# The GLU product of a state-space branch as three split products, and a reordered turn between two phases of an attention stage

## Chip, cores and metric

The kernel runs on one core of one Trainium2 chip. The metric is device time in microseconds, from the start of the one launch to its end. Three runs of the kernel before took 1898.04, 1898.96 and 1899.64 us (median 1898.96).

## What is computed

One layer of a decoder trunk over 2048 tokens with D_MODEL = 1024. An input projection feeds three causal mixers (pooling, forgetting attention with 8 heads of 64, a complex-diagonal state-space layer), each with its own gate; they are merged with sigmoid gates, projected and normalised.

```python
z = einsum('bsd,de->bse', x, w_in) + b_in      # zc: state branch; q, k, v, f: attention; zg: merge gates
# state branch, u = zc (256 channels)
y = Re(C x_t) + D * u                          # x_t = Abar x_{t-1} + Bbar u_t, 16 groups of 16 channels
y = gelu(y)
y_c = y * sigmoid(y @ w_glu + b_glu) * silu(gc)         # w_glu: 256 x 256
# attention, per head
p = softmax(q k^T / 8 + F[t] - F[s], causal);  y_b = (p @ v) * silu(gb)
gates = sigmoid(zg);  merged = sum_i gates_i * (y_i @ w_up_i)
out = layer_norm(2**0.25 * x + merged @ w_out)
```

## The kernel before

All products on TensorE (PE) that matter are split products: each fp32 operand is written as a high part in fp32r (ScalarE, ACT, copies and rounds) and a low part in fp32r (VectorE, DVE, subtracts), and high*high, high*low and low*high are added in PSUM. The low part lies where the raw fp32 operand lay (`low_with_raw`).

**Stage 1, projection** (`stage_project`, to 599 us). The tokens are taken in two halves of 1024 (`hf`), 24 weight tiles of 128 columns each. A tile is 48 matmuls of 128x512 (8 depth blocks, 3 split products, 2 banks). Two PSUM tiles, two weight buffers. Between the tiles PE does small products for the side branches, in PSUM banks `aux_ps`. At the end of a half, for the state branch: `y` products, a tile, 16 transposes into `yT` (which lies over `u_sb`), a tile, then `glu()` (L897 to L907), which multiplies `w_glu` with `yT` in plain fp32, 8 matmuls of 128x512. ACT applies GELU (L398) to `yT` before that. In the first half the tile ahead of `glu()` is the last one that reads the first half of x, so x of the second half is loaded, split by ACT (L355) and DVE (L451) at the same time. In the second half one tile follows `glu()` (`project_halves`).

**Stage 2, attention** (`stage_attend`, 600 to 1529 us). A loop over 8 heads. Every head is one written-out order on PE (`head`): `queries` (q k^T of one block of 128 queries into `s_ps`), `turn` (128x128 transposes of the weights `s_sb` into `t_ps`), `values` (times v into `o_ps`), and between them `fill`: matmuls of the gate projection, 6 tiles of 48 per head, so 24 tiles in 4 heads. Heads 0 to 3 (phase 0) take the gate tiles of one half of the tokens, heads 4 to 7 (phase 1) those of the other. At the change of phase x of the other half is loaded again (SP, L1249) and split again: ACT L1387, DVE L1504, 16 pieces of 128x512 each. In the first tile of phase 1 PE waits for each depth block of x_lo (`fresh`, in `fill`). A head begins with q k^T of block 0 and the transposes of v (L1629, into both `t_ps`). ACT then splits gate weights (L1346), copies the high part of v (L1394), and takes the exponential of block t (L1400) once DVE has the negated row maximum (L1464). DVE splits weights (L1434), makes the low part of v (L1513), then `logits`. `turn(0)` on PE waits for the exponential of block 0 and for the first low part of v.

**Stage 3, merge** (`stage_merge`, from 1529 us) is not touched.

Each engine runs its own instruction list; order between engines is by semaphores. SP issues most DMAs, GpSimd (POOL) those of q, k, v, f and of the mixers' outputs.

Of the kernel before, what the change touches and what calls it, by code (L numbers as in the profile page):

```python
# [25 lines left out]
P = 128  # L26
# [119 lines left out]
def stage_project(nc, io, scr, kept, ident, x_hi, x_lo, x_raw, w_hi, w_lo, w_raw):  # L146


    with ExitStack() as ctx:
        def sb(name, shape, dt=F32):  # L150
            return ctx.enter_context(nc.sbuf_tensor(name, shape, dt))

        def sem(name):
# [16 lines left out]

        zs = sb("zs", [P, 2, HALF])
        zs_flat = zs[:].rearrange("p j n -> p (j n)")
# [3 lines left out]
        yT = u_sb[:].rearrange("p g c -> p (g c)").rearrange("p (j t) -> p j t", j=2)  # L176
        xs = sb("xs", [P, GROUPS, CHUNKS + 1])
        xw = kept.xw
# [14 lines left out]
        sgn = sb("sgn", [P, 2])  # L193
        glu_w = sb("glu_w", [P, 2, D_C])
        glu_b = sb("glu_b", [P, 2])
# [14 lines left out]
         disc_act, disc_arg, coefs, in_table, out_table, kern_ready, toep_set,  # L210
         pooled, v_ready, zc_out, zc_stored, u_loaded, scanned, glu_in, glu_sig, glu_out, yT_in, gelu_done, f_arg, f_exp, f_ln,
         f_done, f_stored) = (
# [3 lines left out]
                "pool_stored", "glu_stored", "dve_step", "pool_step", "x_used", "disc_act", "disc_arg", "coefs", "in_table", "out_table", "kern_ready", "toep_set", "pooled",  # L216
                "v_ready", "zc_out", "zc_stored", "u_loaded", "scanned", "glu_in", "glu_sig", "glu_out", "yT_in", "gelu_done", "f_arg",
                "f_exp", "f_ln", "f_done", "f_stored"))
# [100 lines left out]
        def _(act):  # L319
            def split_w(par, loaded):  # L320

                act.wait_ge(w_loaded[par], loaded)
                act.activation(w_hi[par][:], w_raw[par][:], ACT.Copy).then_inc(w_split_hi, 1)  # L323
# [33 lines left out]
            for hf in range(2):  # L357
# [52 lines left out]
        def _(dve):  # L410
# [144 lines left out]
            for hf in range(2):  # L555
# [110 lines left out]
                def next_split(back):  # L666

                    split_w(back % 2, n0 + T_HALF - back + 2)

                def glu_combine():  # L670
                    for i in range(4):
                        ps = bank("glu", hf, i)
                        dve.tensor_scalar(glu_v[:, i // 2, (i % 2) * BANK:(i % 2 + 1) * BANK], ps[:],
                                          glu_b[:, i // 2:i // 2 + 1], None, ALU.add).then_inc(glu_in, 1)
                        dve.wait_ge(glu_in, 4 * hf + i + 1)
                        dve.nop().then_inc(aux_free, 1)
                    for e in range(2):
                        dve.wait_ge(glu_sig, 2 * hf + e + 1)
                        dve.tensor_tensor(glu_v[:, e, :], glu_v[:, e, :], yT[:, e, :], ALU.mult).then_inc(glu_out, 1)
# [29 lines left out]
                if hf == 0:  # L709
                    split_x(range(1))  # L710
                    tile_from_end(1)
                    split_x(range(1, KT))
                    next_split(1)
                    glu_combine()
                else:
                    tile_from_end(2)
                    glu_combine()
                    next_split(2)
                    dve.wait_ge(z_stored[1], 8 * 2 * (T_SIL + T_QKV) - 16)
                    for c in range(NCH):  # L720
                        cols = slice(c * BANK, (c + 1) * BANK)
                        dve.wait_ge(tile_done, 2 * T_HALF + c)
                        dve.tensor_scalar(zout[1][:, cols], tile_ps[1][:, cols], bias[:, T_HALF - 1:T_HALF], None,
                                          ALU.add).then_inc(tile_out, 1)

        @block.tensor
        def _(pe):
# [91 lines left out]
            for hf in range(2):  # L819
# [78 lines left out]
                def glu():  # L898
                    pe.wait_ge(gelu_done, 2 * (hf + 1))
                    for i in range(4):  # L900
                        ps = open_bank("glu", hf, i)
# [234 lines left out]
def stage_attend(nc, io, scr, kept, ident, mask, x_hi, x_lo, x_raw, gw_hi, gw_lo, gw_raw):  # L1136
# [4 lines left out]
    with ExitStack() as ctx:  # L1141
# [65 lines left out]
        def _(sp):  # L1207
# [17 lines left out]
            for phase in range(2):  # L1225
# [16 lines left out]
                for u in range(2):  # L1242
                    for c in range(NCH):
# [11 lines left out]
                        if phase == 1 and u == 0 and c == 1:  # L1255
# [22 lines left out]
                    if phase == 0:  # L1278
# [53 lines left out]

        def phases(eng, before, body):
            for phase in range(2):
                before(phase)
                with eng.Fori(0, PHASE_HEADS - phase) as i:

                    body(lambda k, c: i * k + (c + phase * PHASE_HEADS * k), lambda k, c: i * k + c, False)
            body(lambda k, c: (HEADS - 1) * k + c, lambda k, c: (PHASE_HEADS - 1) * k + c, True)

        @block.scalar
        def _(act):
# [22 lines left out]
            def high_wu(i):  # L1365
                act.activation(kept.wu_hi[:, KT - 1 - i], kept.early_raw[:, i], ACT.Copy).then_inc(kept.wu_high, 1)
# [6 lines left out]

            def before(phase):
                if phase == 0:
                    split_kq(64)
                    act.sem_inc(gw_split_hi, 1)
                    act.wait_ge(gb_loaded, 16)
                    act.activation(g_bias[:], g_bias[:], ACT.Copy, scale=0.5).then_inc(gb_half, 1)
                    act.wait_ge(gb_half, 1)  # L1380
                else:
                    act.wait_ge(g_done, NCH * T_GATE)
                    for c in range(NCH):
                        for k in range(KT):
                            cols = slice(c * BANK, (c + 1) * BANK)
                            act.wait_ge(x2_loaded[c][k // 2], 16)
                            act.activation(x_hi[:, k, cols], x_raw[:, k, cols], ACT.Copy).then_inc(x2_hi, 1)  # L1387

            def body(at, in_phase, last):
                for j in splits("head", last):  # L1390
# [6 lines left out]
                for t in range(Q_TILES):  # L1397
                    act.wait_ge(max_ready, at(Q_TILES, t + 1))
                    row = s_sb[t % 2][:, 0:(t + 1) * P]
                    act.activation(row, row, ACT.Exp, bias=neg_max[t % 2][:],  # L1400
                                   accum_out=row_sum[:, t:t + 1]).then_inc(p_ready, 1)
                    gates(at, in_phase, (t, 0), last)
# [25 lines left out]
            phases(act, before, body)  # L1428

        @block.vector  # L1430
        def _(dve):
# [60 lines left out]

            def before(phase):
                if phase == 0:
                    dve.sem_inc(gw_split, 1)
                    split_kq(2)
                    for u in range(2):
                        dve.wait_ge(kept.z_stored[u], 8 * 2 * (T_SIL + T_QKV))
                else:
                    for c in range(NCH):  # L1500
                        for k in range(KT):
                            cols = slice(c * BANK, (c + 1) * BANK)
                            dve.wait_ge(x2_hi, c * KT + k + 1)
                            dve.tensor_tensor(x_lo[:, k, cols], x_raw[:, k, cols], x_hi[:, k, cols].bitcast(F32),  # L1504
                                              ALU.subtract).then_inc(x2_split, 1)

            def body(at, in_phase, last):
                for j in splits("head", last):
                    split_w(at, j)
                for b in range(2):  # L1510
# [3 lines left out]
                                      v8[:, :, 0:HD].bitcast(F32), ALU.subtract).then_inc(t_lo, 1)  # L1514
                dve.wait_ge(f_loaded, at(16, 16))
                logits(at, 0)
                for t in range(Q_TILES):
# [25 lines left out]
                for j in splits("tail", last):  # L1543
                    split_w(at, j)

            phases(dve, before, body)

# [670 lines left out]
```

## Time and profile before

| | |
|---|---|
| median of 3 runs | 1898.96 us |
| profiled execution | 1898.0 us |
| its span, first to last instruction | 1896.4 us |
| PE busy | 1878.7 us (99%) |
| DVE busy | 1121.5 us (59%) |
| ACT busy | 722.2 us (38%) |
| POOL busy | 451.0 us (24%) |

The profiled execution lies 1.6 us over its span and 1.0 us under the median. PE is covered almost without a gap: the 40 slices of the page show PE at nine tenths or more in 39, and a granted clock of nine tenths or more in all. A matmul's duration in the rows contains its pipeline, so two consecutive ones overlap; what one costs is read from start to start.

### The profile page before, as it was taken

The page shows a single profiled execution, that of the slowest core. Times are in us where ns is not written, and L with a number is a line of the kernel's source. Part 1 is how long each engine was busy: PE and PEld are TensorE (multiplying, and loading weights), DVE is VectorE, ACT ScalarE, POOL GpSimd, SP SyncE. Part 2 cuts the span into 40 slices and gives each one's busy share as a digit, 9 for nine tenths or more (in the row PEclk, how much of TensorE's full clock was granted, in tenths as well). Part 3 has the DMA queues.
Part 4 walks back from the last instruction along what each step waited for, and adds up shares of the span by engine and source line. Part 5 has one row for each costly group of instructions (what it writes and reads, how often), then busy time and mean ns, then how long its engine had stood idle before and what let it go on. Part 6 is the DMA issues. An engine that isn't in the chain of part 4 may idle for free. (4 is left out here: it accounts for less than half of the span.)

```text
span 1896.4 us, 30753 instructions
## 1 busy us (share of the span) xinstructions
PE 1878.7 (99%) x10349; PEld 1610.2 (85%) x10349; DVE 1121.5 (59%) x2370; ACT 722.2 (38%) x1106; POOL 451.0 (24%) x595
## 2 busy tenths in 40 slices
PE   9999999999999999999999999999999999999998
PEld 7887887888887888888888788888888889999997
DVE  5554225564235665746556675665656688766776
ACT  3121013111024565555655655555555542121111
POOL 2948920399000000010100001000010002233322
PEclk9999999999999999999999999999999999999999
DMA  7132235322432243161432715224162487566542
GB/s 198 67 101 90 88 111 189 78 89 89 151 128 100 63 131 82 46 158 57 126 82 66 230 51 140 71 82 127 49 159 69 163 281 213 179 186 180 167 132 89
DMA packets 111337, 230.24 MB, mean 121 GB/s; under 512 B 11544, under 2 KB 61320, under 8 KB 107640
## 3 DMA queue, kind: packets, MB, share of 16 engines
q1 hardware_dynamic: 96752, 168.69, 27.9%
q0 software_dynamic: 13920, 59.46, 11.8%
q10 hardware_dynamic: 576, 1.05, 0.2%
q8 instruction: 38, 0.62, 0.1%
q14 instruction: 51, 0.42, 0.1%
HBM read 159.29 MB, written 69.27 MB: 121 GB/s over the span
## 5 line engine op out<-in xcount | busy, mean ns | idle before, releaser
L1612 PE MATMUL g_ps<-x_hi,w_hi 128*128 128x512 f32 x768 | 305.5, 398 | 0.0
L1612 PE MATMUL g_ps<-x_hi,w_lo 128*128 128x512 f32 x768 | 305.2, 397 | 0.0
L1530 DVE TENSOR_TENSOR pt_lo<-t_ps,pt_hi 128x512 fp32r<-128x512 f32 (+2 forms) x320 | 193.2, 610 | 148.6 <-ACT pt_hi L1409 144.3
L1612 PE MATMUL g_ps<-x_lo,w_hi 128*128 128x512 f32 x768 | 230.4, 404 | 2.1 <-PEq L1648 1.2
L1409 ACT ACTIVATE pt_hi<-t_ps 128x512 fp32r<-128x512 f32 (+2 forms) x320 | 170.6, 533 | 144.2 <-PE t_ps L1568 138.4
L763 PE MATMUL tile_ps<-x_hi,w_hi 128*128 128x512 f32 x720 | 223.6, 392 | 0.0
L763 PE MATMUL tile_ps<-x_hi,w_lo 128*128 128x512 f32 x720 | 221.7, 389 | 0.0
L763 PE MATMUL tile_ps<-x_lo,w_hi 128*128 128x512 f32 x720 | 221.7, 389 | 0.0
L1303 POOL DMA_DIRECT2D mixT<-y_out x63 | 33.8, 537 | 678.0 <-DVE y_out L1473 604.6
L1568 PE MATMUL t_ps<-ident,s_sb 128*128 128x128 f32 x1088 | 173.1, 274 | 1.5 <-ACT s_sb L1400 1.5
L1450 DVE CUSTOM_DVE_ANT_0 s_sb<-s_ps,f_row 128x512 f32<-128x512 f32 (+3 forms) x288 | 161.2, 597 | 15.2 <-PE s_ps L1557 15.2
L323 ACT ACTIVATE w_hi<-w_lo_raw 128x1024 fp32r<-128x1024 f32 x47 | 49.8, 1060 | 312.1 <-DMA w_lo_raw<-in_w_tiles 312.1
L1612 PEld LDWEIGHTS g_ps<-x_hi,w_lo 128*128 128x128 f32 x768 | 144.6, 188 | 25.2
L1612 PEld LDWEIGHTS g_ps<-x_hi,w_hi 128*128 128x128 f32 x768 | 144.7, 188 | 24.6
L1568 PEld LDWEIGHTS t_ps<-ident,s_sb 128*128 128x128 f32 x1088 | 131.8, 140 | 35.2 <-issue 4.1
L763 PEld LDWEIGHTS tile_ps<-x_hi,w_hi 128*128 128x128 f32 x720 | 134.6, 188 | 29.0 <-issue 1.4
L763 PEld LDWEIGHTS tile_ps<-x_hi,w_lo 128*128 128x128 f32 x720 | 135.2, 188 | 28.2
L763 PEld LDWEIGHTS tile_ps<-x_lo,w_hi 128*128 128x128 f32 x720 | 135.2, 188 | 28.1
L1400 ACT ACTIVATE s_sb<-s_sb,neg_max 128x128 f32<-128x128 f32 (+15 forms) x128 | 153.3, 1198 | 13.0 <-DVE neg_max L1464 13.0
L1612 PEld LDWEIGHTS g_ps<-x_lo,w_hi 128*128 128x128 f32 x768 | 136.3, 189 | 24.1 <-PEq L1648 1.3
L2047 PE MATMUL u_ps<-y_hi,wu_hi 128*128 128x256 f32 x512 | 144.0, 281 | 1.2 <-PEq L1141 0.8
L2047 PE MATMUL u_ps<-y_lo,wu_hi 128*128 128x256 f32 x512 | 144.4, 282 | 0.0
(319 smaller groups left out, 3593.2 us busy)
## 6 DMA issues: line engine op xcount, KB each, us to landing
w_lo_raw<-in_w_tiles SPq DMA_DIRECT2D x95, 512.0 KB, 3.7
gateT<-g_out SPq DMA_DIRECT2D x96, 256.0 KB, 3.0
gate<-gateT SPq DMA_DIRECT2D x62, 384.0 KB, 4.8
qkvT<-zout SPq DMA_DIRECT2D x24, 512.0 KB, 3.2
x_lo_raw<-in_xT SPq DMA_DIRECT2D x20, 512.0 KB, 8.8
silT<-zout SPq DMA_DIRECT2D x16, 512.0 KB, 2.7
k_ll<-qkvT POOLq DMA_DIRECT2D x16, 512.0 KB, 7.5
q_st<-qkvT POOLq DMA_DIRECT2D x16, 512.0 KB, 9.2
```

Source lines behind the costliest of these rows:

```text
L323: act.activation(w_hi[par][:], w_raw[par][:], ACT.Copy).then_inc(w_split_hi, 1)
L763: last = pe.matmul(tile_ps[par][:, c * BANK:(c + 1) * BANK], w[par][:, k, :], x[:, k, c * BANK:(c + 1) * BANK], start=(k == 0 and j == 0), ...
L1303: pool.dma_start(scr["mixT"][bass.ds(row, HD), p * 2 * P:(p + 1) * 2 * P], y_out[p % 2]).then_inc(y_stored, 16)
L1400: act.activation(row, row, ACT.Exp, bias=neg_max[t % 2][:], accum_out=row_sum[:, t:t + 1]).then_inc(p_ready, 1)
L1409: act.activation(pt_hi[:, k0 // P:(k0 + keys) // P, (t % 2) * P:(t % 2 + 1) * P], t_ps[n % 2][:, 0:keys].rearrange("p (k q) -> p k q", q=P ...
L1450: return dve.tensor_tensor_reduce(s_sb[t % 2][:, k0 + a:k0 + b], s_ps[n % 3][:, a:b], f, 1.0, -3e38, ALU.subtract, ALU.max, mx[t % 2][:, c ...
L1530: dve.tensor_tensor(pt_lo[part], t_ps[n % 2][:, 0:keys].rearrange("p (k q) -> p k q", q=P), pt_hi[part].bitcast(F32), ALU.subtract).then_i ...
L1568: last = pe.transpose(t_ps[n % 2][:, a * P:(a + 1) * P], s_sb[t % 2][:, k0 + a * P:k0 + (a + 1) * P], ident[:])
L1612: mm = pe.matmul(g_ps[c][:], w[j % 2][:, k, :], x[:, k, c * BANK:(c + 1) * BANK], start=(r == 0), stop=(r == 3 * KT - 1))
L2047: mm = pe.matmul(u_ps[d % 2][:, n, :], w, y[:, k, :], start=(k == k0 and j == 0), stop=(k == k1 - 1 and j == 2))
```

## The change

Two parts.

*GLU.* `w_glu` and `yT` are split into high and low fp32r parts, and `glu()` adds three split products per fp32 product, 24 matmuls for 8. ACT makes `y_hi` (one copy of 2048 elements per partition), DVE makes `y_lo`, and in the first half also both parts of `w_glu`. PE's wait is now on DVE's `y_split` where it was on ACT's `gelu_done`. `y_hi` takes the place of `zs`, so the results of the GLU product are read out only after all four banks are done.

*Turn.* PE's list is the same as before. ACT and DVE split x of the new half within the body of head 3: ACT 8 pieces, the last gate activation, 8 pieces, each half with its own wait; DVE all 16 after its last work of the head. In every head the logits and the exponential of block 0 come ahead of the splits of weights and v. SP loads the last gate weights ahead of the last gate store.

```diff
-        zs = sb("zs", [P, 2, HALF])
+        y_hi, zs = low_with_raw(nc, ctx, "glu_y_hi", [P, 2, HALF])
-        xs = sb("xs", [P, GROUPS, CHUNKS + 1])
+        y_lo, xs = low_with_raw(nc, ctx, "glu_y_lo", [P, GROUPS, CHUNKS + 1])
-        glu_w = sb("glu_w", [P, 2, D_C])
+        glu_lo, glu_w = low_with_raw(nc, ctx, "glu_lo", [P, 2, D_C])
+        glu_hi = sb("glu_hi", [P, 2, D_C], F32R)
 # stage 1, ACT, after GELU
                 if hf == 0:
                     split_w(0, 8 * T_HALF + 16)
+                act.wait_ge(gelu_done, 2 * (hf + 1))
+                act.activation(y_hi[:], yT, ACT.Copy).then_inc(y_high, 1)
+                if hf == 0:
                     split_x(range(KT))
 # stage 1, DVE
+                def split_yT():
+                    if hf == 0:
+                        dve.wait_ge(consts, n_consts)
+                        link(dve.tensor_copy(glu_hi[:], glu_w[:]))
+                        dve.tensor_tensor(glu_lo[:], glu_w[:], glu_hi[:].bitcast(F32), ALU.subtract)
+                    dve.wait_ge(y_high, hf + 1)
+                    dve.tensor_tensor(y_lo[:, :, 1:], u_sb[:], y_hi[:].bitcast(F32).rearrange("p j (g t) -> p (j g) t", t=CHUNKS),
+                                      ALU.subtract).then_inc(y_split, 1)
                 def glu_combine():
+                    bank("glu", hf, 3)
...
                 if hf == 0:
                     split_x(range(1))
+                    split_yT()
                     tile_from_end(1)
...
                 else:
+                    split_yT()
                     tile_from_end(2)
 # stage 1, PE
-                    pe.wait_ge(gelu_done, 2 * (hf + 1))
+                    pe.wait_ge(y_split, hf + 1)
...
-                            last = pe.matmul(ps[:], glu_w[:, j, e * P:(e + 1) * P], yT[:, j, c * BANK:(c + 1) * BANK],
-                                             start=(j == 0), stop=(j == 1))
+                            for n, (w, y) in enumerate(((glu_hi, hi), (glu_lo, hi), (glu_hi, y_lo[:, chunks, 1:]))):
+                                last = pe.matmul(ps, w[:, j, e * P:(e + 1) * P], y, start=(j == 0 and n == 0),
+                                                 stop=(j == 1 and n == 2))
 # stage 2, SP: the last weight load of phase 0 moves ahead of the store of bank 1
+                        if phase == 0 and u == 1 and c == 1:
+                            sp.wait_ge(g_done, (m0 + T_GATE - 1 + u) * 2)
+                            load_w((T_HALF + u) * P, u)
 # stage 2, ACT
+            def high_x(c):
+                act.wait_ge(g_done, NCH * T_GATE - NCH + c + 1)
+                for k in range(KT):
+                    cols = slice(c * BANK, (c + 1) * BANK)
+                    act.wait_ge(x2_loaded[c][k // 2], 16)
+                    act.activation(x_hi[:, k, cols], x_raw[:, k, cols], ACT.Copy).then_inc(x2_hi, 1)
+            def body(at, in_phase, last=False, turn=False):
+                def weights_of(t):
+                    act.wait_ge(max_ready, at(Q_TILES, t + 1))
+                    row = s_sb[t % 2][:, 0:(t + 1) * P]
+                    act.activation(row, row, ACT.Exp, bias=neg_max[t % 2][:],
+                                   accum_out=row_sum[:, t:t + 1]).then_inc(p_ready, 1)
+
+                weights_of(0)
                 for j in splits("head", last):
                     split_w(at, j)
...
+                if turn:
+                    high_x(0)
                 gates(at, in_phase, "tail", last)
+                if turn:
+                    high_x(1)
 # stage 2, DVE
+            def body(at, in_phase, last=False, turn=False):
+                dve.wait_ge(f_loaded, at(16, 16))
+                logits(at, 0)
                 for j in splits("head", last):
                     split_w(at, j)
...
+                if turn:
+                    for c in range(NCH):
+                        low_x(c)
```

In place of two loops (heads 0 to 3, heads 4 to 6) and a head written out, ACT and DVE now run a loop over heads 0 to 2, head 3 written out, a loop over heads 4 to 6 and head 7 written out.

VectorE at the end of the first half of stage 1, before, from the split of the next tile's weights on:

```order
L421 TENSOR_TENSOR w_lo<-w_lo_raw,w_hi 128x1024
L451 TENSOR_TENSOR x_lo<-x_lo_raw,x_hi 128x1024
L663 TENSOR_SCALAR zout_94<-tile_ps,bias 128x1024
L451 TENSOR_TENSOR x_lo<-x_lo_raw,x_hi 128x1024 x7
L421 TENSOR_TENSOR w_lo<-w_lo_raw,w_hi 128x1024
L673 TENSOR_SCALAR zs<-aux_ps,glu_b 128x512 x4
```

VectorE at the same place now (`glu_lo_raw` is `glu_w`, `glu_y_hi_raw` is `zs`):

```order
L425 TENSOR_TENSOR w_lo<-w_lo_raw,w_hi 128x1024
L455 TENSOR_TENSOR x_lo<-x_lo_raw,x_hi 128x1024
L677 CAST glu_hi<-glu_lo_raw 128x512
L678 TENSOR_TENSOR glu_lo<-glu_lo_raw,glu_hi 128x512
L680 TENSOR_TENSOR glu_y_lo<-u_sb,glu_y_hi 128x16x128
L667 TENSOR_SCALAR zout_94<-tile_ps,bias 128x1024
L455 TENSOR_TENSOR x_lo<-x_lo_raw,x_hi 128x1024 x7
L425 TENSOR_TENSOR w_lo<-w_lo_raw,w_hi 128x1024
L687 TENSOR_SCALAR glu_y_hi_raw<-aux_ps,glu_b 128x512 x4
```

Three instructions stand between the first piece of x_lo and the read-out of the tile, and PE's GLU product waits for the third.

ScalarE at the change of phase, before, from the last gate activation of head 3 to the v copies of head 4:

```order
L1357 ACTIVATE g_out_102<-g_ps,g_bias 128x512
L1336 REGISTER_ALU
L1336 COMPARE_AND_BRANCH
L1387 ACTIVATE x_hi<-x_lo_raw 128x512 x16
L1336 UNCONDITIONAL_BRANCH
L1336 ISA
L1346 ACTIVATE w_hi<-w_lo_raw 128x1024
L1393 ISA
L1394 ACTIVATE v_st<-t_ps 128x8x64
```

ScalarE at the same place now:

```order
L1411 ACTIVATE x_hi<-x_lo_raw 128x512 x8
L1382 ACTIVATE g_out_102<-g_ps,g_bias 128x512
L1411 ACTIVATE x_hi<-x_lo_raw 128x512 x8
L1362 UNCONDITIONAL_BRANCH
L1362 ISA
L1417 ACTIVATE s_sb_95,row_sum<-s_sb_95,neg_max_3777 128x128
L1370 ISA
L1371 ACTIVATE w_hi<-w_lo_raw 128x1024
L1424 ISA
L1425 ACTIVATE v_st<-t_ps 128x8x64
```

Eight pieces of x_hi stand ahead of the gate activation, and the exponential of block 0 (`s_sb_95`) stands ahead of the weight split and the copies of v.

## Rows read from the trace of the kernel before

**Rows 1.** The page, part 1: busy us (share of the span) xinstructions

```profile
PE 1878.7 (99%) x10349; PEld 1610.2 (85%) x10349; DVE 1121.5 (59%) x2370; ACT 722.2 (38%) x1106; POOL 451.0 (24%) x595
```

**Rows 2.** Waits of PE: engine, line, releaser; us in total, times, longest

```profile
PE t_ps L1568 <- ACT s_sb L1400: 1.5, 1, 1.5
PE g_ps L1612 <- DVE x_lo L1504: 0.9, 1, 0.9
```

**Rows 3.** Timeline, PE at the first GLU product: start us, us, instruction

```profile
300.49 7.03 PE L904 MATMUL aux_ps<-u_sb,glu_w 128*128 128x512 f32 x16
...
307.82 0.63 PE L763 MATMUL tile_ps<-x_hi,w_lo 128*128 128x512 f32 x2
...
319.63 0.62 PE L763 MATMUL tile_ps<-x_hi,w_hi 128*128 128x512 f32 x2
```

**Rows 4.** Timeline, ACT and DVE ahead of the first GLU product

```profile
294.28 1.06 ACT L398 ACTIVATE u_sb<-u_sb 128x1024 f32<-128x1024 f32 x1 [1.51 <-DVE u_sb L705]
295.25 1.04 ACT L323 ACTIVATE w_hi<-w_lo_raw 128x1024 fp32r<-128x1024 f32 x1
...
298.43 1.23 DVE L451 TENSOR_TENSOR x_lo<-x_lo_raw,x_hi 128x1024 fp32r<-128x1024 f32 x1 [0.88 <-ACT x_hi L355]
...
301.89 8.03 DVE L451 TENSOR_TENSOR x_lo<-x_lo_raw,x_hi 128x1024 fp32r<-128x1024 f32 x7
```

**Rows 5.** Groups by form: xcount | busy us, mean ns | idle before, releaser

```profile
L1370 ACT ACTIVATE k_hh<-k_ll 128x2048 fp32r<-128x2048 f32 x8 | 15.2, 1904 | 9.2 <-PEq L149 9.2
...
L1487 DVE TENSOR_TENSOR k_ll<-k_ll,k_hh 128x2048 fp32r<-128x2048 f32 x8 | 18.3, 2293 | 15.4 <-ACT k_hh L1370 15.4
...
L548 DVE COPY xs<-aux_ps 128x512 f32<-128x512 f32 x8 | 5.5, 691 | 0.2
...
L1504 DVE TENSOR_TENSOR x_lo<-x_lo_raw,x_hi 128x512 fp32r<-128x512 f32 x16 | 9.7, 685 | 2.6 <-ACT x_hi L1387 2.6
```

**Rows 6.** Timeline, ACT and PE at the second GLU product

```profile
574.20 2.01 ACT L398 ACTIVATE u_sb<-u_sb 128x1024 f32<-128x1024 f32 x2
...
580.88 7.03 PE L904 MATMUL aux_ps<-u_sb,glu_w 128*128 128x512 f32 x16
```

**Rows 7.** Timeline, PE at the change of phase

```profile
1065.12 0.47 PE L1612 MATMUL g_ps<-x_lo,w_hi 128*128 128x512 f32 x1 [0.92 <-DVE x_lo L1504]
...
1075.94 0.39 PE L1612 MATMUL g_ps<-x_hi,w_hi 128*128 128x512 f32 x1
1077.87 0.32 PE L1568 MATMUL t_ps<-ident,s_sb 128*128 128x128 f32 x1 [1.55 <-ACT s_sb L1400]
```

**Rows 8.** Timeline, ACT at the change of phase

```profile
1060.20 0.38 ACT L1363 ACTIVATE o_low<-o_ps 64x256 f32<-64x256 f32 x1
...
1063.63 8.43 ACT L1387 ACTIVATE x_hi<-x_lo_raw 128x512 fp32r<-128x512 f32 x16
1072.58 1.06 ACT L1346 ACTIVATE w_hi<-w_lo_raw 128x1024 fp32r<-128x1024 f32 x1 [0.53 <-DMA w_lo_raw<-in_w_tiles]
...
1077.25 0.40 ACT L1400 ACTIVATE s_sb<-s_sb,neg_max 128x128 f32<-128x128 f32 x1 [2.05 <-DVE neg_max L1464]
```

**Rows 9.** Timeline, DVE at the change of phase

```profile
1076.26 0.28 DVE L1442 TENSOR_TENSOR f_last<-f_row,mask 128x128 f32<-128x128 f32 x1
```

**Rows 10.** Timeline, SP: the loads of x, second half of the banks

```profile
1059.28 2.00 SPq L1249 DMA_DIRECT2D x_lo_raw<-in_xT  x4
```

**Rows 11.** DMA issues between 1060.8 and 1061.3 us: count, KB, us to landing

```profile
x_lo_raw<-in_xT SPq DMA_DIRECT2D x1, 512.0 KB, 9.6
```

**Rows 12.** Timeline, PE at the start of an ordinary head (head 1)

```profile
723.15 1.20 PE L1629 MATMUL t_ps<-ident,vT 64*128 64x64 f32 x16
...
728.50 0.27 PE L1568 MATMUL t_ps<-ident,s_sb 128*128 128x128 f32 x1
```

**Rows 13.** Windows at the end: us, busy by engine (x), PEclk, DMA share, GB/s

```profile
1888.00:1889.00 1.00, 0.23 (x2) 0.00 (x0) 0.66 (x1) 0.00 (x0) 0.31 (x1) 1.00 0.00 0
...
1891.00:1892.00 1.00, 0.00 (x0) 0.00 (x0) 0.93 (x3) 0.00 (x0) 0.00 (x0) 0.58 0.00 0
```

More of the change, by code:

```diff
@@ L898, in glu @@
                 def glu():
[L899 removed]
+                    pe.wait_ge(y_split, hf + 1)
                     for i in range(4):
[L901 removed]
+                        ps = open_bank("glu", hf, i)[:].rearrange("p (g t) -> p g t", t=CHUNKS)
                         e, c = i // 2, i % 2
                         for j in range(2):
[L904 to L905 removed]
+                            chunks = slice(8 * j + 4 * c, 8 * j + 4 * c + 4)
+                            hi = y_hi[:, j, c * BANK:(c + 1) * BANK].rearrange("p (g t) -> p g t", t=CHUNKS)
+                            for n, (w, y) in enumerate(((glu_hi, hi), (glu_lo, hi), (glu_hi, y_lo[:, chunks, 1:]))):
+                                last = pe.matmul(ps, w[:, j, e * P:(e + 1) * P], y, start=(j == 0 and n == 0),
+                                                 stop=(j == 1 and n == 2))
                         last.then_inc(aux_full, 1)
@@ L1277, in _ @@
                                          ).then_inc(kept.free_loaded, 16)
-                    if phase == 0:
+                    if phase == 0 and u == 0:
                         sp.wait_ge(g_done, (m0 + T_GATE - 1 + u) * 2)
@@ L1331, in _, with phases @@
                     store_inv((HEADS - 1) * 9, (HEADS - 1) * HD, 2, 2)
[L1333 to L1339, printed above, removed]
+        def phases(eng, begin, body):
+            begin()
+            with eng.Fori(0, PHASE_HEADS - 1) as i:
+                body(lambda k, c: i * k + c, lambda k, c: i * k + c)
+            body(lambda k, c: (PHASE_HEADS - 1) * k + c, lambda k, c: (PHASE_HEADS - 1) * k + c, turn=True)
+            with eng.Fori(0, PHASE_HEADS - 1) as i:
+                body(lambda k, c: i * k + (c + PHASE_HEADS * k), lambda k, c: i * k + c)
+            body(lambda k, c: (HEADS - 1) * k + c, lambda k, c: (PHASE_HEADS - 1) * k + c, last=True)
         @block.scalar
@@ L1372, in split_kq, with begin @@
                 act.activation(q_st[0:HD], q_st[0:HD].bitcast(F32), ACT.Copy, scale=HD ** -0.5).then_inc(q_hi, 1)
[L1374 to L1389, printed above, removed]
+            def begin():
+                split_kq(64)
+                act.sem_inc(gw_split_hi, 1)
+                act.wait_ge(gb_loaded, 16)
+                act.activation(g_bias[:], g_bias[:], ACT.Copy, scale=0.5).then_inc(gb_half, 1)
+                act.wait_ge(gb_half, 1)
+            def high_x(c):
[11 more added lines that the diff above has]
+                weights_of(0)
                 for j in splits("head", last):
@@ L1397, in body @@
                 for t in range(Q_TILES):
[L1398 to L1401, printed above, removed]
+                    if t:
+                        weights_of(t)
                     gates(at, in_phase, (t, 0), last)
@@ L1425, in body @@
                     high_wu(EARLY_SPLIT - 1)
+                if turn:
+                    high_x(0)
                 gates(at, in_phase, "tail", last)
-            phases(act, before, body)
+                if turn:
+                    high_x(1)
+            phases(act, begin, body)
         @block.vector
@@ L1491, in split_kq, with begin, low_x @@
                                          ALU.mult, ALU.subtract).then_inc(kq_low, 1)
[L1493 to L1507, printed above, removed]
+            def begin():
+                dve.sem_inc(gw_split, 1)
+                split_kq(2)
+                for u in range(2):
+                    dve.wait_ge(kept.z_stored[u], 8 * 2 * (T_SIL + T_QKV))
+            def low_x(c):
+                for k in range(KT):
+                    cols = slice(c * BANK, (c + 1) * BANK)
+                    dve.wait_ge(x2_hi, c * KT + k + 1)
+                    dve.tensor_tensor(x_lo[:, k, cols], x_raw[:, k, cols], x_hi[:, k, cols].bitcast(F32),
+                                      ALU.subtract).then_inc(x2_split, 1)
+            def body(at, in_phase, last=False, turn=False):
+                dve.wait_ge(f_loaded, at(16, 16))
+                logits(at, 0)
                 for j in splits("head", last):
@@ L1544, in body @@
                     split_w(at, j)
-            phases(dve, before, body)
+                if turn:
+                    for c in range(NCH):
+                        low_x(c)
+            phases(dve, begin, body)
         @block.tensor
```

6 lines of the change are left out of this document (2 added, 4 removed).

## The prediction

> **What bounds the kernel now.** I read the page's busy shares first: TensorE is busy 1878.7 of 1896.4 us, no other engine over 60% [rows 1]. So only three things can move the time: what TensorE itself executes, what it waits for, and new waits that the change gives it. Then the list of its waits. Only two lie where the change works, both at the change of phase: 0.9 us for x_lo and 1.5 us for the first exponential [rows 2]. Then the timeline of TensorE at the two places that the diff touches [rows 3, 6, 7], and the timelines of the engines that will feed it there [rows 4, 6, 8, 9]. The reader is to see that ScalarE and VectorE have much idle time in all, but that at these places they stand close ahead of TensorE.
>
> **TensorE's own work in the GLU product.** The fp32 product starts at 300.49 and the second pair of the tile behind it at 307.82 [rows 3]. From 307.82 to 319.63 there are 26 pairs of split matmuls, so one costs 11.81 / 52 = 0.227 us. Without its first pair (0.45) the tile behind would begin at 307.37, so the 8 fp32 matmuls cost 6.88 us. Now they are 24 split ones: 24 x 0.227 = 5.45 us. That takes off 1.43 us per half, 2.9 us in all. Each of the 24 has weights of its own, as every matmul of rows 3 has, so the price holds. The low part of y is read in four runs of 128, which no row shows; by the nearest row it costs the same, and if those 8 matmuls per half ran at the fp32 pace (6.88 / 8 = 0.86) the saving would turn into a loss of 3.6 us per half. I take the first.
>
> **The wait in front of it, first half.** Now TensorE waits for y_lo on VectorE. The chain: the second GELU ends at 295.34, the weight split behind it at 296.29 [rows 4]. The copy y_hi of 2048 elements costs 1.90 as k_hh does [rows 5]: 298.2. ScalarE then makes the first piece of x_hi, 1024 elements, 1.04 as the weight split: 299.2. VectorE has the first piece of x_lo ahead of the three new instructions and must wait for it: 1.23 [rows 4], 300.45. Then glu_hi (a copy of 512; nearest a PSUM copy, 0.69), glu_lo (a subtract of 512, 0.69) and y_lo (a subtract of 2048, 2.29) [rows 5]: 304.1. TensorE would like to begin at 300.49. New wait: 3.6 us. Nothing hides it: the queue of TensorE is in order, and the next tile, whose operands would be ready, stands behind the GLU product. With glu_hi at nothing it is 2.9. With y_lo, written around a gap at each 129th element, at twice its price, it is 5.9. I keep 3.6: all but glu_hi have a row of the same size.
>
> The VectorE page of the Trainium skill ("VectorE: DVE Perf Modes", section "Mode 2×_2P — use both read ports for one tensor") says that an fp32 copy within SBUF runs at twice the rate of a two-operand operation. By it glu_hi would take about 0.35 and the wait would be 3.3 us. No row here has such a copy.
>
> What is behind the three instructions on VectorE: the read-out of a tile (1.28 of work) and 7 pieces of x_lo, 8.03 for all [rows 4], which move from 301.9 to about 305.4. TensorE starts its next tile at 304.1 + 5.45 = 309.6 and needs a piece only every 6 x 0.227 = 1.36 us, slower than the 1.15 in which VectorE makes one. So this costs nothing more. The read-out of the GLU banks now waits for the fourth; the banks are next needed two tiles later (96 x 0.227 = 21.8 us), so nothing.
>
> **Second half.** GELU ends at 576.21 [rows 6], y_hi 578.1, y_lo 580.4. w_glu is split already and no x is split here. TensorE arrives at 580.88. No wait, with 0.5 us to spare; at worst, with y_lo at twice its price, 1.8 us.
>
> **The change of phase.** TensorE lost 0.92 at 1065.12, and at 1077.87 the difference between 1075.94 + 0.23 and 1077.87, that is 1.70 [rows 7]. So 2.6 us are the most that can be won. The first goes: ScalarE began the 16 x_hi pieces at 1063.63 only because it waited for the last gate matmuls; now it begins behind o_low, which ends at 1060.58 [rows 8], and x_lo is ahead of TensorE. The second is what comes late next. I follow the chain from the DMA. The last load of x is issued at 1060.8 and lands 9.6 us later, at 1070.4 [rows 10, 11]; that issue hangs on TensorE and does not move. Two pieces of x_hi at 8.43 / 16 = 0.53 [rows 8]: 1071.5. The last x_lo, 0.6: 1072.1. Logits of block 0 up to the start of the exponential, 1077.25 - 1076.26 = 1.0 [rows 8, 9]: 1073.1. The exponential with its read-out of the sum, 0.6: 1073.7. The weights have landed by 1072.5 even in the old place [rows 8], so w_hi follows, 1.06: 1074.8. VectorE's w_lo, 1.23: 1076.0. The low part of v, 512 elements, 0.68: 1076.7. The hops between engines add perhaps 0.1 to 0.3. TensorE, without the first wait, would come at 1075.25, so it waits about 1.6 us again, now for v_lo and not for the exponential, and goes on at 1076.9 instead of 1077.87. I take a gain of 1.0, between nothing (each hop dearer) and 2.6 (w_lo and v made early).
>
> In an ordinary head of phase 0 the same order of ScalarE and VectorE follows the queries. They end just ahead of the v transposes at 723.15; logits 1.0, exponential 0.6, w_hi 1.06, w_lo 1.23 and v_lo 0.68 give 727.7, and TensorE's first transpose stands at 728.50 [rows 12]. It keeps 0.8 us. In phase 1, 30 more matmuls (6.8 us) lie between. So nothing, in seven heads.
>
> **Sum.** -2.9 + 3.6 + 0.0 - 1.0 = -0.3 us. The profiled execution of 1898.0 becomes 1897.7; it lies 1.0 under the median of 1898.96, so the median becomes **1898.7 us**. About 0.2% (3.8 us) is what a measurement of this kernel can tell from no change, so this is none.
>
> **Rivals.**
> *The wait drops TensorE's clock.* The last matmul ends at 1888.23 (0.23 busy in that window), and between 1891 and 1892 the granted clock is 0.58, from its upper level (2.4 GHz) to its lower one (1.2 GHz): it fell 2.9 us after TensorE went idle [rows 13]. The new gap of 3.6 us is longer than that. Against it: the waits of rows 2 are all short, so no row shows a gap in mid-kernel. If it falls, the GLU product that follows runs wholly or partly at half speed: up to 5.4 us, and 2 if it recovers before half of it is over. With 2 the time is 1900.7. The Trainium skill ("TensorE: Matmul & The Clock Gate", section "Why this matters for your kernels") warns that an idle gap between bursts of matmuls brings the clock back to its lower level; by that rule it would fall here, and the one case in the trace agrees.
> *The heads lose their margin.* The w_hi of each head now stands behind the exponential, which waits for VectorE, which waits for the queries and f. If the margin of 0.8 us in rows 12 is used up by hops or by a late weight landing, four heads wait, each some 1 us: +4, 1902.7 us, slower than before. It decides from about 0.2 us more per step of that chain of five. Against it: every step has a row.
> *The turn gives all.* If x lands earlier now, since a gate store leaves the queue ahead of the weights, v_lo could be there when TensorE arrives: 1.6 more, and with the short copy 0.3 more: 1896.8.
> *The wait in the first half is not there.* If VectorE's three instructions found y_hi ready and the weights cheap, the GLU part alone would win 2.9: 1895.1. Rows 4 speak against it: TensorE is ready at 300.49 and the first x_lo alone ended at 299.66 in the old order.
>
> **Chances.** The forecast's case 0.50, its own range 1897.5 to 1900.0 (0.7 on the wait, 1.0 on the turn). The clock 0.27. The heads or a dearer y_lo 0.10. The full turn 0.09. No wait 0.04. Range: 1896.5 to 1902.0; it leaves out half of the heads' case, the clock with the full 5.4 (0.04) and the last case, 0.13 in all. Faster by over 0.2% (under 1895.2): 0.04. Slower by over 0.2% (over 1902.8): 0.09, from the heads' case and the clock with a full 5.4. Within: 0.87.
>
> **What would show it.** In the profile of the changed kernel: the GLU matmuls 0.227 us apart, 24 in a row; a wait of PE for y_lo of 3 to 4 us in the first half, at about 300 us, and none or under 0.5 us in the second; the granted clock in the 5 us behind that wait; at the change of phase no wait for x_lo, and one of 1 to 2 us whose releaser is the low part of v; no wait of PE at the first transposes of the other heads. The prediction fails if one of the two new chains is off by more than 3 us, or if a wait comes up in the ordinary heads.

## The result: 3.6 us slower, and the profile after

| | before | after |
|---|---|---|
| median | 1898.05 us (1897.22 to 1899.82, 20 runs) | 1901.61 us (1899.81 to 1906.21, 20 runs) |
| ratio | | 1.0018, 95% interval 1.0012 to 1.0025 |
| profiled execution, its span | 1898.0, 1896.4 | 1900.16, 1898.2 |

The time lies in the forecast range, but 2.9 us above the forecast: the change made the kernel a little slower, where no difference was forecast. The forecast started from a median of three runs, 1898.96, which lies 0.9 over the median of 20; held against that one, a change of -0.3 was forecast and +3.6 measured. The runs after also lie further apart, and in steps: 7 at 1899.8 to 1900.6, nine at 1901.4 to 1902.7, three at 1903.3 to 1904.4, one at 1906.2. The mean granted clock of TensorE, recorded for each run to three digits, falls along with these steps: 0.998 in eight runs (1899.8 to 1901.6), 0.997 in nine (1901.4 to 1903.3), 0.996 in two (1903.4 and 1904.4), 0.995 in the last (1906.2). The profiled execution belongs to the lowest step. Its busy times answer to [rows 1]:

```profile
PE 1876.7 (99%) x10365; PEld 1613.9 (85%) x10365; DVE 1126.1 (59%) x2374; ACT 723.7 (38%) x1107; POOL 450.2 (24%) x595
```

TensorE is busy 2.0 us less, in a span that is 1.8 us longer. Its waits (engine, line, releaser; us in total, times, longest), to be held against [rows 2]:

```profile
PE tile_ps L762 <- DVE x_lo L444: 3.0, 2, 1.6
PE aux_ps L923 <- DVE glu_y_lo L680: 3.0, 1, 3.0
PE aux_ps L72 <- PEq L2166: 2.4, 1, 2.4
PE g_ps L1647 <- PEq L1683: 1.9, 1, 1.9
PE t_ps L1603 <- DVE v_st L1547: 1.6, 1, 1.6
```

Three lines matter: the new wait for y_lo; the stop ahead of the first gate product of stage 2, which was 1.16 us before; and the wait at the change of phase, now for the low part of v. The other two stand at the start of the program, where the kernel before has 1.6 and 2.4 us. The stop ahead of stage 2 was in the list of the kernel before too, but not among [rows 2], so the prediction never priced it:

```profile
PE g_ps L1612 <- PEq L1648: 1.2, 1, 1.2
```

The first GLU product, with the timelines of ACT, DVE and PE (start, us, instruction, idle before it and releaser), answers to [rows 3, 4]:

```profile
296.63 1.90 ACT L403 ACTIVATE glu_y_hi<-u_sb 128x2048 fp32r<-128x2048 f32 x1
...
299.51 1.23 DVE L455 TENSOR_TENSOR x_lo<-x_lo_raw,x_hi 128x1024 fp32r<-128x1024 f32 x1 [1.52 <-ACT x_hi L356]
300.65 0.42 DVE L677 CAST glu_hi<-glu_lo_raw 128x512 fp32r<-128x512 f32 x1
301.10 0.69 DVE L678 TENSOR_TENSOR glu_lo<-glu_lo_raw,glu_hi 128x512 fp32r<-128x512 f32 x1
301.71 2.28 DVE L680 TENSOR_TENSOR glu_y_lo<-u_sb,glu_y_hi 128x2048 fp32r<-128x2048 f32 x1
304.05 0.50 PE L923 MATMUL aux_ps<-glu_y_hi,glu_hi 128*128 128x512 f32 x1 [2.96 <-DVE glu_y_lo L680]
...
309.55 0.40 PE L923 MATMUL aux_ps<-glu_y_lo,glu_hi 128*128 128x512 f32 x1
309.78 0.61 PE L779 MATMUL tile_ps<-x_hi,w_hi 128*128 128x512 f32 x2
```

The three DVE instructions take one after the other what the forecast gave them, but for the copy (0.42 instead of 0.69). The product fills 304.05 to 309.78: 5.73 us for 24 matmuls, 0.239 each with the hand-over to the next tile, against 6.88 before. The second one and the seam to stage 2:

```profile
580.52 2.29 DVE L680 TENSOR_TENSOR glu_y_lo<-u_sb,glu_y_hi 128x2048 fp32r<-128x2048 f32 x1 [2.10 <-ACT glu_y_hi L403]
583.27 0.39 PE L923 MATMUL aux_ps<-glu_y_hi,glu_hi 128*128 128x512 f32 x1
...
589.10 0.75 DVE L687 TENSOR_SCALAR glu_y_hi_raw<-aux_ps,glu_b 128x512 f32<-128x512 f32 x1 [4.34 <-PE aux_ps L923]
...
595.73 0.53 POOL L1052 DMA_DIRECT2D mixT<-glu_y_hi_raw  x1 [0.59 <-DVE glu_y_hi_raw L693]
...
602.27 3.44 PE L1647 MATMUL g_ps<-x_lo,w_hi 128*128 128x512 f32 x8 [1.88 <-PEq L1683]
```

TensorE does not wait for the second y_lo. But now the read-out begins when all four banks are done, and the last store of the GLU result is issued at 595.73. The kernel before has for that store and for the start of stage 2:

```profile
591.88 0.53 POOL L1033 DMA_DIRECT2D mixT<-zs  x1 [0.60 <-DVE zs L679]
...
600.43 2.10 PE L1612 MATMUL g_ps<-x_lo,w_hi 128*128 128x512 f32 x8 [1.16 <-PEq L1648]
```

The two store issues lie 3.85 us apart; 1.15 of it is what TensorE itself is behind by then, so against TensorE's list the store is 2.7 us later. The same eight matmuls that took 2.10 take 3.44 after. The windows of the kernel after show why (us, busy by engine (x), PEclk, DMA share, GB/s):

```profile
602.00:603.00 1.00, 0.73 (x3) 0.60 (x4) 0.00 (x0) 1.00 (x1) 0.00 (x0) 0.84 0.43 172
603.00:606.00 3.00, 3.00 (x9) 2.32 (x8) 2.29 (x1) 2.95 (x3) 0.00 (x0) 0.50 0.87 296
606.00:607.00 1.00, 1.00 (x6) 0.84 (x5) 0.97 (x2) 1.00 (x1) 0.00 (x0) 0.95 0.00 0
```

From 602.7 to 606.1 the granted clock is 0.50, the lower of its two levels. It is the only such fall in mid-kernel in this execution; behind the longer wait at 304 the clock stayed at 1.00. The change of phase answers to [rows 7 to 9]:

```profile
1077.09 0.41 ACT L1417 ACTIVATE s_sb<-s_sb,neg_max 128x128 f32<-128x128 f32 x1 [1.72 <-DVE neg_max L1497]
1077.49 1.04 ACT L1371 ACTIVATE w_hi<-w_lo_raw 128x1024 fp32r<-128x1024 f32 x1
1078.57 1.23 DVE L1467 TENSOR_TENSOR w_lo<-w_lo_raw,w_hi 128x1024 fp32r<-128x1024 f32 x1 [1.51 <-ACT w_hi L1371]
1079.72 1.28 DVE L1547 TENSOR_TENSOR v_st<-t_ps,v_st 128x512 fp32r<-128x512 f32 x2
1080.45 0.33 PE L1603 MATMUL t_ps<-ident,s_sb 128*128 128x128 f32 x1 [1.64 <-DVE v_st L1547]
```

Laid side by side, the two profiled executions drift apart as follows (starts of the same work; each line holds all the difference up to it; 307.37 and 587.75 are, as in the prediction, the start of the tile's next matmuls less one price, since the first one overlaps the fp32 product):

| place | before | after | difference | step |
|---|---|---|---|---|
| TensorE ready for the first GLU product | 300.49 | 300.93 | +0.44 | +0.4, start of the program |
| tile behind it | 307.37 | 309.78 | +2.41 | wait +3.1, product -1.15 |
| second GLU product | 580.88 | 583.27 | +2.39 | 0 |
| tile behind it | 587.75 | 588.90 | +1.15 | product -1.24 |
| stage 2 | 600.43 | 602.27 | +1.84 | seam +0.7 |
| loads of x, second half | 1059.28 | 1062.75 | +3.47 | clock +1.6 |
| first exponential's transpose | 1077.87 | 1080.45 | +2.58 | change of phase -0.9 |
| span | 1896.4 | 1898.2 | +1.8 | -0.8, 0.5 of it at the first product of stage 3 |

### The profile page after: what moved, and what is told of

It reads as the page before. It is cut to its first block and busy times, and to the rows that moved or that the text cites. A ratio compares the mean times of both kernels' runs of the same rounds, so it can differ in the third digit from the quotient of the medians.

```text
span 1898.2 us, 30572 instructions
## 1 busy us (share of the span) xinstructions
PE 1876.7 (99%) x10365; PEld 1613.9 (85%) x10365; DVE 1126.1 (59%) x2374; ACT 723.7 (38%) x1107; POOL 450.2 (24%) x595
```

## Experiments

Theory A: TensorE's clock falls in some executions behind its gaps, and the change adds and lengthens gaps. Theory B: waits and prices alone explain it. Every kernel was timed beside the kernel before, whose medians there were 1897.8 to 1897.9; of its 89 runs 68 have a mean granted clock of 0.999 and 21 of 0.998.

| run | kernel | median (range, runs) us | ratio (95%) |
|---|---|---|---|
| e1 | turn only | 1897.35 (1896.86 to 1899.13, 11) | 0.9999 (0.9990 to 1.0008) |
| e2 | GLU only | 1902.33 (1900.29 to 1906.78, 7) | 1.0026 (1.0015 to 1.0037) |
| e3 | first GLU half split | 1900.39 (1898.09 to 1903.80, 11) | 1.0014 (1.0005 to 1.0023) |
| e4 | second GLU half split | 1897.80 (1896.06 to 1900.57, 11) | 1.0000 (0.9991 to 1.0009) |
| e5 | gaps filled | 1898.88 (1897.84 to 1899.75, 11) | 1.0004 (0.9995 to 1.0013) |
| e6 | early splits | 1897.45 (1895.87 to 1899.66, 11) | 0.9997 (0.9988 to 1.0006) |
| e7 | results outside y_hi | 1899.92 (1898.57 to 1901.83, 11) | 1.0009 (1.0000 to 1.0019) |
| e8 | v before the weights | 1901.21 (1900.52 to 1903.40, 11) | 1.0018 (1.0009 to 1.0027) |
| e9 | all mended | 1893.41 (1892.67 to 1894.20, 11) | 0.9976 (0.9967 to 0.9985) |
| e10 | e9 with the GLU in fp32 | 1895.68 (1894.86 to 1897.58, 11) | 0.9990 (0.9981 to 0.9999) |
| e11 | e9 with a longer seam filling | 1893.67 (1892.72 to 1894.37, 11) | 0.9978 (0.9969 to 0.9987) |

**The parts.** e1 is the kernel before with the edits of `stage_attend` alone, e2 with those of `stage_project` alone. e3 and e4 keep both, but leave one half's GLU product in fp32:

```diff
 # e3; e4 has hf == 0 for hf == 1
-                    pe.wait_ge(y_split, hf + 1)
+                    if hf == 1:
+                        pe.wait_ge(gelu_done, 2 * (hf + 1))
+                    else:
+                        pe.wait_ge(y_split, 1)
...
```

> The reordered turn alone, GLU product in fp32 as before. Both theories: the wait at the change of phase falls from two (0.9 + 1.7 us) to one of about 1.6 us behind v_lo, so 0.9 us less than before, ratio 0.9995. Theory A (the clock falls in gaps of TensorE that the GLU part opens or lengthens): mean granted clock as before, 0.999 in most runs. Theory B (the loss is in steady prices: the wait in front of the first GLU product, slower matmuls, dearer heads): if the heads are dearer, it shows here as more than before.

> The split GLU product alone, turn as before. Theory A: +0.9 us against the changed kernel, so about 1902.5 us or +4.4 against before, in steps of 1.7 us from run to run, with mean clocks of 0.998 to 0.996. Theory B: the same mean, but without steps, and with a mean clock of 0.999.

> Changed kernel, but with the GLU product of the second half in fp32 as before; w_glu keeps a place of its own. The wait of 3 us in the first half stays, the seam between stages 1 and 2 is as before. Theory A: the clock falls at the seam as seldom as before (idle 1.2 us there again), and in some runs in the 3 us gap: +1.1 us against before without a fall, +2.8 with one; mean between. Theory B: +2.3 us or more, without steps.

> Changed kernel, but with the GLU product of the first half in fp32 as before; the split of w_glu is done in the second half ahead of y_lo. No gap at 300 us. Theory A: the late read-out of the GLU banks makes GpSimd late at the seam between the stages; idle there 1.9 us for 1.2, the clock falls there in most runs: -1.4 us against before without the fall, +0.3 with it. Theory B (first wait is the loss): -2 us against before in every run, idle at the seam 1.2 us.

The loss is the GLU part's, and in it the first half's: e2 takes 4.5 us more than the kernel before; e3 takes 3.0 more than e1, which has the same turn, and e4 0.45 more, which the intervals can't tell from nothing. e1 itself came out 0.4 faster than before where 0.9 was expected, also within its interval, and only 5 of its 11 runs have a mean clock of 0.999. e3's median, 2.6 over before, fits both theories. Its runs fit theory A: the three with a mean clock of 0.999 took 1898.1 to 1899.5, the two longest (1903.0 and 1903.8) have 0.997. e4 fits A better than B, which had 2 us less than before and a seam of 1.2 us: its seam is 1.9, and its two longest runs (1900.2 and 1900.6) have 0.997. In its profile e3, whose seam is 1.2 us as before, has a low clock behind the wait at 304:

```profile
303.00:304.00 1.00, 0.48 (x2) 0.38 (x3) 1.00 (x2) 0.81 (x1) 0.00 (x0) 0.86 0.97 377
304.00:306.00 2.00, 2.00 (x6) 1.61 (x5) 2.00 (x3) 1.59 (x3) 0.00 (x0) 0.50 0.85 336
306.00:308.00 2.00, 2.00 (x8) 1.52 (x8) 2.00 (x3) 1.82 (x2) 0.00 (x0) 0.72 0.48 195
308.00:310.00 2.00, 2.00 (x10) 1.63 (x9) 2.00 (x3) 1.30 (x2) 0.00 (x0) 1.00 0.00 0
```

Six records in two microseconds at the low level, ten at the high one. e2 has two falls in its profile, at 305.3 and, behind a wait of 4.0 us for the exponential, at 1083.5: that wait is the old order of the change of phase, with weights that landed late (11.0 us after their issue, 8.4 in the profile before). e1 has one, behind the wait of 2.0 us for the low part of v. e1's timeline of PE and its windows:

```profile
1077.68 0.33 PE L1584 MATMUL t_ps<-ident,s_sb 128*128 128x128 f32 x1 [2.01 <-DVE v_st L1528]
```

```profile
1077.00:1078.00 1.00, 0.32 (x2) 0.33 (x3) 1.00 (x3) 0.30 (x1) 0.00 (x0) 1.00 0.00 0
1078.00:1079.00 1.00, 1.00 (x5) 0.91 (x4) 0.97 (x7) 0.28 (x1) 0.00 (x0) 0.50 0.63 240
1079.00:1081.00 2.00, 2.00 (x6) 1.54 (x6) 1.28 (x8) 1.18 (x3) 0.00 (x0) 0.50 0.03 11
```

The matmul that stands at 1077.87 in the profile before is 0.2 us earlier in e1, the one at 1081.61 is 1.4 us later (1082.99), so the low clock costs 1.6 us there. Behind the wait for y_lo it costs 1.5: the 24 matmuls fill 7.27 us in e3 (303.52 to 310.79) and 5.73 in after. Not every execution has a fall: e1's profiled one took 1898.66, and 8 of its 11 runs took 1896.9 to 1897.9. e4 has none in its profile, and its median is that of before: the second half wins 1.24 in the product and gives some of it back at the seam.

**The gaps filled (e5).** The waits stay; TensorE multiplies into a bank that nobody reads meanwhile:

```diff
+                    if hf == 0:
+                        keep_warm(pe, open_bank("glu", 0, 0), ident, 9)
                     pe.wait_ge(y_split, hf + 1)
...
-            keep_warm(pe, tile_ps[0], ident, WARM_END)
+            keep_warm(pe, tile_ps[0], ident, WARM_END + 4)
```

> Changed kernel, with dummy matmuls on the identity in two gaps of TensorE: 9 ahead of the wait for the first y_lo (about 2.4 of the 3.0 us), 4 more at the end of stage 1 (about 1.1 us of the 1.9). No wait is shortened and nothing else moves. Theory A (the clock falls in the gaps): no fall at 304 or 602 us, so the median drops by 1.7 to 3 us to about 1898.7 to 1899.5, mean clock 0.999 in most runs. Theory B (the waits as such are the loss): median as the changed kernel, 1901.6.

The median, 1898.88, is as theory A expected, 2.7 us under the kernel after. All 11 runs lie under all 20 of after, and the spread falls from 6.4 to 1.9. The mean clock is 0.999 in seven and 0.998 in four of them, where after has 0.999 in none. Its timeline of PE at the first GLU product, and its windows there and at the seam:

```profile
300.39 2.17 PE L72 MATMUL aux_ps<-ident 128*128 128x128 f32 x18
...
303.52 0.50 PE L925 MATMUL aux_ps<-glu_y_hi,glu_hi 128*128 128x512 f32 x1 [0.95 <-DVE glu_y_lo L680]
```

```profile
304.00:306.00 2.00, 2.00 (x11) 1.58 (x10) 2.00 (x3) 1.65 (x2) 0.00 (x0) 1.00 0.89 350
...
603.00:606.00 3.00, 3.00 (x15) 2.49 (x14) 2.79 (x2) 2.95 (x3) 0.00 (x0) 1.00 0.64 224
```

No useful work begins earlier in this kernel: from the first dummy matmul at 300.39 to the GLU product are 3.13 us, and after has 3.12 from 300.93 on; from the first dummy matmul of the seam to stage 2 both have 2.49. Yet the time is lower: this is the run that speaks for theory A and against B.

**The waits taken away (e6, e7).** e6 makes the weight split early and the y split ahead of x_lo. e7 puts the second half's GLU result into the free space of `toep`, so that its read-out need not wait for the fourth bank:

```diff
@@ e6, stage_project, VectorE @@
+                    link(dve.tensor_copy(glu_hi[:], glu_w[:]))   # behind the "y" read-out
+                    dve.tensor_tensor(glu_lo[:], glu_w[:], glu_hi[:].bitcast(F32), ALU.subtract)
...
-                    split_x(range(1))
                     split_yT()
+                    split_x(range(1))
@@ e7, stage_project @@
+        glu_place = [glu_v, toep[:].rearrange("p g c -> p (g c)").rearrange("p (e t) -> p e t", e=2)]
...
-                    bank("glu", hf, 3)
+                    if hf == 0:
+                        bank("glu", hf, 3)
```

> Changed kernel, with the split of w_glu put ahead of the tile read-outs, where VectorE idles, and y_lo ahead of the first piece of x_lo. The wait for the first y_lo should go from 3.0 us to 0 to 0.3. Theory A: -3.0 and the falls at 304 us with it, so -3.5 or so, about 1898.0, the seam still at 1.9 us and falling in many runs. Theory B: -3.0 exactly.

> Changed kernel, with the GLU results of the second half in the place of toep, so that each bank is read out as soon as it is full. Theory A (GpSimd's last stores make it late at the seam, since the read-out began only after the fourth bank): idle at the seam 1.2 us for 1.9 and the falls there mostly gone, -0.7 to -2 us. Rival: the seam stays at 1.9 us (something else in the second half makes it late, the copies of y on ScalarE or VectorE).

Both came out as theory A expected: e6 4.2 us under after (3.5 or so expected, 3.0 by theory B), e7 1.7 us under it (0.7 to 2). e6 has no wait for y_lo. Its seam is still 1.88 us, and the clock fell there in its profile, from 599.2 to 602.6; with that fall it took 1896.67. e7 has its seam back at 1.16 us and keeps the wait of 3.0, and the clock fell there, from 305.3 to 308.7. Start of stage 2 in e7, and in e4, which has the late read-out:

```profile
603.53 2.09 PE L1649 MATMUL g_ps<-x_lo,w_hi 128*128 128x512 f32 x8 [1.16 <-PEq L1685]
```

```profile
600.19 2.10 PE L1661 MATMUL g_ps<-x_lo,w_hi 128*128 128x512 f32 x8 [1.88 <-PEq L1697]
```

The seam is 1.16 to 1.2 in before, e1, e3, e7, e9 and e10, and 1.88 to 1.9 in after, e2, e4, e6 and e8: long just where the read-out waits for the fourth bank. e11 (0.8) and e5 (1.0) have more dummy matmuls ahead of it, which fill the stop and do not shorten it. What the start of stage 2 hangs on shows in all 13 profiles. In after, e2, e4, e5, e6 and e8 it comes 6.53 to 6.54 us after GpSimd issues the last store of the GLU result (593.65 and 600.19 in e4), and 3.3 us after that store has landed. In the seven others that store is 8.5 to 9.0 us ahead, and stage 2 begins 1.6 us after the start of VectorE's last read-out of a tile (601.97 and 603.53 in e7).

**The change of phase (e8).** The v parts stand ahead of the weights, on ScalarE and VectorE alike:

```diff
-                for j in splits("head", last):
-                    split_w(at, j)
                 # v_hi on ScalarE, v_lo on VectorE
+                for j in splits("head", last):
+                    split_w(at, j)
```

> Changed kernel, with the copies and low parts of v ahead of the split of the gate weights at the head of each head, on ScalarE and VectorE. Both theories: the wait of 1.6 us at the change of phase goes to 0 to 0.3 us, as w_hi (1.06) and w_lo (1.23) leave the chain. Theory A: -1.5 us and up to 0.8 more for falls at 1080 us. Theory B: -1.5.

A miss. The wait for v_lo is 0.5 instead of 1.6, but the weights' low part is now late, and TensorE stops two microseconds later for that:

```profile
1078.84 0.33 PE L1603 MATMUL t_ps<-ident,s_sb 128*128 128x128 f32 x1 [0.54 <-DVE v_st L1545]
...
1080.88 2.10 PE L1647 MATMUL g_ps<-x_lo,w_hi 128*128 128x512 f32 x8 [1.13 <-DVE w_lo L1467]
```

The two waits make 1.67: the gap was moved, not shortened.

**Together (e9, e10, e11).** e9 is e6 and e7 with ScalarE's weight copy ahead of the exponential (VectorE's order stays). e10 is e1 with that same edit, so the GLU is in fp32. e11 is e9 with two more dummy matmul groups at the seam.

```diff
+                for j in splits("head", last):
+                    split_w(at, j)
                 weights_of(0)
-                for j in splits("head", last):
-                    split_w(at, j)
```

> Changed kernel with three things put right: w_glu split early and y_lo ahead of x_lo (as in the run with early splits), GLU results of the second half in the place of toep, and at the head of each head ScalarE's split of the gate weights ahead of the exponential of block 0, in the time in which it waits for the logits. Theory A: no gap at 300 us, idle 1.2 us at the seam, 0 to 0.6 us at the change of phase; without falls 1898.5 - 3.0 - 0.7 - 1.3 = 1893.5, median 1893.5 to 1895. If the falls were not tied to the gaps, the median would stay 1.5 to 3 us above 1893.5 with mean clocks of 0.998 and 0.997.

> The mended turn alone, GLU product in fp32 as in the kernel before. What the split GLU product is worth once its waits are gone: this kernel should be 2.2 to 2.6 us slower than the fully mended one (two products at 6.9 against 5.7 us), so about 1896; 1.2 us less than the turn alone, whose median was 1897.35.

> The mended kernel with 2 more dummy matmuls (0.5 us) at the end of stage 1. Theory A: a fall at the seam is a little rarer, median 0 to 0.5 us under the mended one. If the seam is bound by TensorE itself, it is up to 0.5 us longer instead.

e9 beats both kernels: 0.24% faster than before, 8.2 us faster than after, and within 0.1 us of the 1893.5 that was expected without falls. Its waits of PE at the seam and the change of phase, and its windows at the three critical places:

```profile
PE g_ps L1648 <- PEq L1684: 1.2, 1, 1.2
...
PE t_ps L1604 <- DVE v_st L1548: 0.6, 1, 0.6
```

```profile
304.00:306.00 2.00, 2.00 (x10) 1.58 (x10) 2.00 (x2) 1.39 (x2) 0.00 (x0) 1.00 1.03 418
603.00:606.00 3.00, 3.00 (x24) 2.57 (x24) 1.65 (x5) 2.69 (x4) 0.00 (x0) 1.00 0.00 0
1078.00:1081.00 3.00, 3.00 (x18) 2.62 (x17) 1.47 (x7) 1.26 (x5) 0.00 (x0) 1.00 0.66 207
```

No wait for y_lo is left, the clock stays up, and 11 runs lie within 1.5 us. e10 is 2.27 us slower than e9; between these two only the GLU product with its splits and its read-out differs, so the split itself is worth about what the matmuls promised (1.15 + 1.24 = 2.4). e11's wait at the seam is 0.8, but only because dummies fill it: from the first of them to stage 2 are 1.84 us, in e9 1.77. It brings no time that the runs can tell.

## Why the prediction was wrong

**Right.** The chain ahead of the first GLU product: 3.6 forecast, 3.0 listed (3.1 from start to start). About half of the difference is the weight copy, 0.42 instead of 0.69. The 0.35 that the prediction took from the Trainium skill ("VectorE: DVE Perf Modes", section "Mode 2×_2P — use both read ports for one tensor") was nearer to the measured 0.42 than the 0.69 of the row. No wait in the second half. At the change of phase the wait for x_lo goes, the next one comes from the low part of v with 1.6 us as forecast, and the place wins 0.9 (forecast 1.0). That it came so near is in part luck: in the seven profiles with this order (after, e1, e3 to e7) the wait is 1.6 to 2.3 us and the place wins 0.3 to 1.0. No ordinary head shows a wait in the profile after. e5's profile has one, 1.1 us for v_lo in the last head (1426.60), where the gate weights landed 8.9 us after their issue, 4.0 in the profile before: that is the rival of the heads, once in these profiles.

**The product itself, a little too dear.** -2.9 forecast, -2.4 measured, since the 24 matmuls take 5.73 and 5.63, not 5.45.

**The step that failed in the sum.** "The read-out of the GLU banks now waits for the fourth; the banks are next needed two tiles later (96 x 0.227 = 21.8 us), so nothing." I asked only who needs the banks. Behind the read-out stand the sigmoid, the product and the last stores, and the second half has a stage seam behind it: that store is issued 2.7 us later against TensorE's list (591.88 and 595.73, less the 1.15 that TensorE is behind), stage 2 waits for it, and TensorE's stop grows from 1.16 to 1.88: +0.7. e7 removes it.

**The choice that failed among the cases.** I gave the clock a chance of 0.27 and took its staying up as the likeliest, so the sum of -0.3 has no term for it, and I looked for a fall at the wait of 3.6 us only. The forecast's terms at their measured size give -2.4 + 3.1 + 0.7 - 0.9 = +0.5. After's lowest runs, with one fall in the profiled one, are 1899.8 to 1900.6; without that fall (1.6) the profiled one would be at about 1898.6, 0.6 above the profiled one before, near what this sum says (the 0.4 at the start of the program and 0.4 outside the span make up for the -0.8 behind the change of phase). The median is 3 us above that. How many falls each timed run had is not recorded, but a fall of 3.4 us to half the clock takes 0.0009 off the mean clock of a run. The median run of after has 0.997, the profiled one, with one fall, 0.998: by that estimate it has about one fall more, two in all, which is 3 us at 1.5 to 1.6 each. The third digit also moves with when the clock falls behind the last matmul (the profiles without a fall have 0.999 or 0.998), and in e5 and e7 it does not put the runs in the order of their times, so it does not count the falls of a single run. That most of these 3 us are falls rests further on e5 (2.7 us from filling alone), on the steps in the run times, and on the low clocks seen in the profiles of after, e1, e2, e3, e6, e7 and e8, and in none of e4, e5, e9, e10 and e11. The rival's price of 2 us was about right (1.4 to 1.6 measured); its place and its count were not.

**Open.** Why a given execution keeps its clock behind a 3 us wait (after's profile, at 304) and the next loses it is not settled. Of the 0.8 us between the change of phase and the end, 0.5 lies at the first product of stage 3 (1549.87 before, 1551.81 after), where TensorE waits 0.4 us for VectorE's `gate` before and not at all after. e2, with the old turn, has no such wait and e8, with the new one, has 0.3, so it goes with neither part of the change; one profile of each kernel can't tell it from scatter.

## What to carry to other kernels

Where TensorE is busy 99% of the span, an added wait costs its length and a chance of a low clock behind it, some 1.4 to 1.6 us a time here. So a split that trades matmul work for a chain on the helper engines pays only if that chain ends before TensorE arrives: against the reordered turn alone the split lost 4.3 us with the chain and the read-out late (1901.61 and 1897.35), and it was worth 2.3 us with both early (1893.41 and 1895.68). And a read-out that is put off must be followed to the next seam of stages, not only to the next use of its banks. Look at the spread of the runs and at their mean clocks: steps that go with lower clocks are a sign of falls where a single profile shows none.

## What the runs showed that I had not expected

- The granted clock fell behind waits of 1.9 to 2.0 us, not only behind those of 3 and 4: at the seam in after and e6 (1.88 in the list, with a few dummy matmuls ahead of it) and in e1 (2.01). Each low stretch in these profiles lasted 3.4 us (303.7 to 307.1 in e3, 1078.0 to 1081.4 in e1, 599.2 to 602.6 in e6).
- The same gap did not always bring it. Behind the wait of 3.0 us the clock was kept in the profile of after and lost in those of e2, e3, e7 and e8; behind the seam of 1.88 us it was lost in after and e6 and kept in e2, e4 and e8.
- A copy of 128x512 from fp32 to fp32r on VectorE took 0.42 us where a subtract of that size took 0.69.
